# A two-layer trunk step on one core: weights loaded a stage ahead, and the second norm in the tail of the expert stage

## The reference

```python
def trunk_layer(x, mod, l, p, ctx):
    sh_a, sc_a, g_a, sh_f, sc_f, g_f = jnp.split(mod, 6, axis=-1)
    h = x * (1.0 + sc_a) + sh_a
    mix, new_ctx = token_mixer(h, l, p, ctx)        # attention, short conv, recurrent scans
    x = layer_norm(ALPHA * x + g_a * mix, ln_g[0], ln_b[0])
    h = x * (1.0 + sc_f) + sh_f
    ff = peer(h, p['peer_wq'], p['peer_keys'], p['peer_u'], p['peer_v'])
    x = layer_norm(ALPHA * x + g_f * ff, ln_g[1], ln_b[1])
    return x, new_ctx
# peer, for each token and each of 8 heads: query = h @ wq; the 16 best of 128*128 experts idx, softmax g;
#   act = gelu(h . u_tab[idx]);  y += sum over the 16 of (g * act) * v_tab[idx]
```

## Time and profile before

| | us |
|---|---|
| median of 3 runs | 7773.9 (7764.08 to 7782.03) |
| the profiled execution | 7747.34 |
| its span | 7745.5 |
| TensorE busy | 5922.2 |
| VectorE busy | 4112.1 |
| GpSimd busy | 2667.7 |
| ScalarE busy | 1916.5 |
| first layer's experts, mixer of layer 2 | from 1900.23; from 3957.68 |

### The profile page before, as it was taken

How to read it: one execution, slowest core, us unless ns; L and a number is a source line. 1 busy time by engine, 2 the same in 40 slices (tenths; PEclk the granted TensorE clock), 3 DMA queues, 4 the chain that set the end, 5 groups by cost and what they waited for, 6 DMA issues and landing times. The chain is left out here.

```text
span 7745.5 us, 97944 instructions
## 1 busy us (share of the span) xinstructions
PE 5922.2 (76%) x37744; PEld 4157.4 (54%) x37744; DVE 4112.1 (53%) x8666; ACT 1916.5 (25%) x3630; POOL 2667.7 (34%) x2848
## 2 busy tenths in 40 slices
PE   4877999786677777777658789997847777777774
PEld 4866999575333333333357679994833333333331
DVE  2358232454666666666445572425456666666664
ACT  1346211231122221222115442113212221222221
POOL 0110000100666666666501100002016666666663
PEclk8998999898899999999879899998979999899997
DMA  5011121014999999999820111110269999999996
GB/s 219 30 38 37 66 77 66 13 74 193 351 364 357 352 348 367 360 353 352 323 109 8 41 56 66 55 66 13 109 249 361 350 362 365 345 364 359 359 353 246
DMA packets 447652, 1659.85 MB, mean 214 GB/s; under 512 B 48552, under 2 KB 92264, under 8 KB 434540
## 3 DMA queue, kind: packets, MB, share of 16 engines
q0 software_dynamic: 368640, 1342.34, 45.6%
q1 hardware_dynamic: 77102, 305.91, 10.5%
q10 hardware_dynamic: 1440, 5.24, 0.2%
HBM read 1638.45 MB, written 20.10 MB: 214 GB/s over the span
## 5 line engine op out<-in xcount | busy, mean ns | idle before, releaser
L1764 PE MATMUL ex_ps_y<-early,peer_small 128*128 128x512 f32 x5120 | 2512.3, 640 | 858.3 <-DMA early<-in_peer_v,ex_index 724.1
L1764 PEld LDWEIGHTS ex_ps_y<-early,peer_small 128*128 128x128 f32 x5120 | 991.1, 203 | 2299.2 <-issue 1221.1
L1673 DVE CUSTOM_DVE_ANT_0 ring<-ring,ex_ps_h 128x1024 f32<-128x1024 f32 x1280 | 1511.1, 1218 | 744.1 <-DMA ring<-in_peer_u,ex_index 598.9
L1582 POOL DMA_INDIRECT ring<-in_peer_u,ex_index x1280 | 1219.4, 953 | 798.9 <-issue 375.3
L1582 POOL DMA_INDIRECT early<-in_peer_v,ex_index x1280 | 1219.1, 952 | 799.8 <-issue 354.5
L1724 ACT ACTIVATE peer_small<-ident,ex_w 128x128 f32<-128x128 f32 x1280 | 444.2, 393 | 1502.6 <-PE ex_ps_y L1764 668.6
L735 POOL TENSOR_TENSOR att_qs<-att_q,ring 128x512 f32<-128x512 f32 x16 | 20.2, 1264 | 1121.0 <-DMA att_lam_in<-in_lam 965.4
L911 POOL TENSOR_TENSOR room<-room,rec_bounds 128x256 f32<-128x256 f32 x80 | 69.7, 872 | 963.2 <-ACT room L905 962.9
L235 PE MATMUL conv_ps<-h_high,conv_wh 128*128 128x320 f32 x1024 | 317.6, 310 | 16.5 <-DVE conv_wl L135 16.5
L1745 PE MATMUL ex_ps_q<-h_high,ex_wh 128*128 128x256 f32 (+1 forms) x768 | 259.3, 338 | 79.8 <-DVE ex_wl L135 45.8
L235 PE MATMUL conv_ps<-h_low,conv_wh 128*128 128x320 f32 x1024 | 317.1, 310 | 0.0
(11 more groups left out here) (314 smaller groups left out, 12428.0 us busy)
## 6 DMA issues: line engine op xcount, KB each, us to landing
ring<-in_w_in SPq DMA_DIRECT2D x44, 2048.0 KB, 8.3
ring<-in_mod_w SPq DMA_DIRECT2D x16, 2048.0 KB, 15.7
ring<-in_w_branch SPq DMA_DIRECT2D x12, 2048.0 KB, 7.8
early<-in_mod_w SPq DMA_DIRECT2D x12, 2048.0 KB, 19.1
ring<-in_peer_u,ex_index POOLq DMA_INDIRECT x1280
early<-in_peer_v,ex_index POOLq DMA_INDIRECT x1280
mod_w<-in_mod_w SPq DMA_DIRECT2D x8, 2048.0 KB, 25.3
room<-in_peer_wq SPq DMA_DIRECT2D x16, 1024.0 KB
```

The source lines that it names most:

```text
L1582: nc.gpsimd.indirect_dma_start(rows[slot], None, table, bass.IndirectOffsetOnAxis(ap=index[n % 4][:, s:s + 1], axis=0)).then_inc(arrived[s ...
L1673: V.tensor_tensor_reduce(out=row, in0=row, in1=ps_h[:], scale=1.0, scalar=0.0, op0=ALU.mult, op1=ALU.add, accum_out=dot[n % 2][:, s:s + 1] ...
L1764: last = nc.tensor.matmul(ps_y[n % 2][:, c:c + 512], diag[s % DIAGS], v_row[s % V_SLOTS][:, c:c + 512], start=s == 0, stop=s == TOPK - 1)
```

## The change

1. **First weights in the stage ahead.** `projections` no longer loads its first chunk: it lies in `ring[0]` when the stage begins, and ACT's first two splits wait for nothing. Each stage ahead gets one load of 2 MB: mt ahead of `rf0` of the first layer (`w_first`, behind the x loads), the two scans (after the state's store and a wait for the 36th of 40 products on DVE), `recm` ahead of `conv` and `conv` ahead of `qkv` (argument `then`), the attention core ahead of `attm` (behind its own loads; these move from `ring[0]` to `ring[1]`), and `experts` ahead of the next layer's `rf0`. Each of these stages waits for the load before its end.
2. **The second norm in the tail of `experts`.** In the last head (units 35 to 39, `FIRST` = 35), `gather_sum` is replaced by `residual(b)`: y added into PSUM, multiplied there by the gate, ALPHA * x added, then statistics and variance of the block. `residual(0)` to `residual(3)` stand in units 36 to 39, `residual(4)` behind everything. x is loaded into the rows of h that are used up, one block per unit, the gate rows when the last query weights are split, the norm's rows after the last score.
3. **The next modulated input in the tail.** Behind the last product DVE normalises and modulates blocks 0 to 2 (`normalised`), then block 4's residual, then blocks 3 and 4; TensorE transposes, ACT copies, DVE subtracts the five blocks (`new_low_of`). The modulation rows are loaded into `ring[1]` after the last product. mt runs once, before the loop.
4. x goes straight to the outputs and is read from there; `copy_rows` is gone, and so is `residual_norm`.

The diff, cut to its core:

```diff
@@ projections
             def _(sp):
-                first = weighted[0].weights
-                for p, (k0, k1) in enumerate(pieces(0)):
-                    sp.dma_start(ring[0][:, k0:k1, 0:HALF], first[:, k0:k1, 0:HALF]).then_inc(first_loaded[p], 16)
-                sp.dma_start(ring[0][:, :, HALF:], first[:, :, HALF:]).then_inc(w_loaded[0], 16)
                 beside.load(sp)
...
                 beside.finish(sp)
+                if then is not None:
+                    sp.wait_ge(low_done, splits(2 * (len(weighted) - 2) + 1))
+                    sp.dma_start(ring[0][:], then).then_inc(next_in, 16)
+                    sp.wait_ge(next_in, 16)
@@ attention_core
-        room = ring[0][:].rearrange("p k n -> p (k n)")
+        room = ring[1][:].rearrange("p k n -> p (k n)")
...
+                sp.dma_start(ring[0][:], w_in(T, l, ZG)).then_inc(k_out, 16)
@@ scan
                 sp.wait_ge(s_done, (blocks.index(CTX_BLOCK) + 1) * HEADS)
                 sp.dma_start(T["new_state"][one, d].rearrange("a p n -> (a p) n"), state_ctx[:]).then_inc(s_out, 16)
-                sp.wait_ge(s_out, 16)
+                sp.wait_ge(x_done, UNITS - G)
+                sp.dma_start(ring[0][:], then).then_inc(s_out, 16)
+                sp.wait_ge(s_out, 32)
@@ experts, SP
+                sp.wait_ge(low_done, PH)
+                for cond in range(2):
+                    sp.dma_start(gate[:, cond, :], mod_row(T, l, cond, 5)).then_inc(gate_in, 16)
+                for b in range(NB):
+                    sp.wait_ge(rows_ready, FIRST + b + 1)
...
+                    sp.dma_start(x_tok[:, b, :], x_from(b)).then_inc(x_in, 16)
+                sp.wait_ge(scored, units)
+                for j, row in enumerate(("ln_g", "ln_b")):
+                    sp.dma_start(gb[:, j, :], ...).then_inc(gb_in, 16)
+                sp.wait_ge(u_used, TOPK * units - U_SLOTS // 2)
+                sp.dma_start(ring[0][:], w_next).then_inc(stored, 16)
+                sp.wait_ge(u_used, TOPK * units)
+                for cond in range(2):
+                    for j in range(2):
+                        sp.dma_start(vec[:, cond, j, :], mod_row(T, l + 1, cond, j)).then_inc(vec_in, 16)
+                for b in range(NB):
+                    sp.wait_ge(x_done, b + 1)
+                    sp.dma_start(x_to(b), x_tok[:, b, :]).then_inc(stored, 16)
+                sp.wait_ge(stored, 16 * (NB + 1))
@@ experts, DVE
+                def residual(b):
+                    x, ps = x_tok[:, b, :], ps_y[(FIRST + b) % 2][:]
...
+                    dve.wait_ge(v_used, TOPK * (FIRST + b + 1))
+                    tail(V.tensor_tensor(ps, ps, y_tok[:, b, :], ALU.add))
+                    tail(V.tensor_tensor(ps, ps, gate[:, b // (NB - 1), :], ALU.mult))
+                    dve.wait_ge(x_in, 16 * (b + 1))
+                    V.scalar_tensor_tensor(x, x, ALPHA, ps, ALU.mult, ALU.add).then_inc(y_out, 1)
...
-                    if n:
+                    if n > FIRST:
+                        residual(n - 1 - FIRST)
+                    elif n:
                         gather_sum(n - 1)
...
-                gather_sum(units - 1)
+                dve.wait_ge(u_used, TOPK * units)
+                dve.wait_ge(vec_in, 64)
+                tail(V.tensor_scalar(vec[:, :, 1, :], vec[:, :, 1, :], 1.0, None, ALU.add))
+                dve.wait_ge(gb_in, 32)
+                inverse(0, 0, 3)
+                for b in range(3):
+                    normalised(b)
+                residual(4)
+                new_low_of(0)
+                inverse(1, 3, 5)
+                normalised(3)
+                new_low_of(1)
+                normalised(4)
+                for b in range(2, NB):
+                    new_low_of(b)
@@ trunk
+        modulate_and_transpose(nc, 0, T, rows, h_split, ident, 0, ring)
         with nc.Fori(0, depth) as l:
-            modulate_and_transpose(nc, l, T, rows, h_split, ident, 0)
...
-                residual_norm(nc, l, T, "ln2", 1, y_tok, x_tok, rows, None, 5, rows)
-        copy_rows(nc, "end", [(T["y_sample"], T["x_rows"][0:LAT, :]), (T["y_prompt"], T["x_rows"][LAT:TOK, :])])
```

More of the change, by code:

```diff
@@ L135, in low_part, with projections @@
     return nc.vector.tensor_tensor(low, full, high.bitcast(F32), ALU.subtract)
-def projections(nc, name, jobs, ring, beside=None):
+def projections(nc, name, jobs, ring, beside=None, then=None):
     beside = beside or Beside()
@@ L949, in recurrent_out @@
         turn = Turn(o_tok, branch_split, beside.column[:, 0:1], ident)
-        projections(nc, "recm", jobs + [gates[0], turn, gates[1]] + products, ring, beside)
+        projections(nc, "recm", jobs + [gates[0], turn, gates[1]] + products, ring, beside, w_in(T, l, ZC))
 class MixerEnd(AttentionBeside):
@@ L1042, in _, with scan @@
                 last.then_inc(rows_done, 1)
-def scan(nc, l, T, d, q_t, i_tok, kk, o_tok, ring, ident):
+def scan(nc, l, T, d, q_t, i_tok, kk, o_tok, ring, ident, then):
     blocks = list(range(NB)) if d == 0 else list(range(NB - 1, -1, -1))
@@ L1509, in _, with experts @@
                 mod.add_bias(summed)
-def experts(nc, l, T, h_split, h_tok, y_tok, early, small, ident, u_in, v_in, ring):
+def experts(nc, l, T, h_split, h_tok, y_tok, early, small, ident, u_in, v_in, ring, x_from, x_to, w_next):
     units = NB * PH
@@ L1545, in experts @@
         iota, base = sb("ex_iota", [P, TOPK]), sb("ex_base", [P, DEPTH])
+        stats, mv, root = sb("ex_stats", [P, NB, 12]), sb("ex_mv", [P, NB, 2]), sb("ex_root", [P, NB])
+        x_tok = h_tok
+        gate, gb = (small[0][:, i * 2 * D:(i + 1) * 2 * D].rearrange("p (a n) -> p a n", a=2) for i in range(2))
+        vec = ring[1][:].rearrange("p k n -> p (k n)").rearrange("p (c j n) -> p c j n", c=2, j=2)
+        h_new = y_tok
+        FIRST = (PH - 1) * NB
         ps_y = [ctx.enter_context(nc.psum_tensor(f"ex_ps_y{j}", [P, D], F32)) for j in range(2)]
@@ L1730, in _ @@
                                 high(h + 2)
+                for b in range(NB):
+                    act.wait_ge(transposed, b + 1)
+                    act.activation(h_split[0][:, :, b * P:(b + 1) * P], new_psum[b % 2][:].rearrange("p (k t) -> p k t", k=KT),
+                                   ACT.Copy).then_inc(new_high, 1)
+                    if b == 0:
+                        act.wait_ge(var_done, 5)
+                        act.activation(root[:, 3:5], mv[:, 3:5, 1], ACT.Sqrt).then_inc(root_done, 1)
             @block.tensor
@@ L1781, in _ @@
                         sums(n, s)
+                for b in range(NB):
+                    pe.wait_ge(h_done, b + 1)
+                    if b == 0:
+                        pe.wait_ge(u_used, TOPK * units)
+                    elif b == 1:
+                        pe.wait_ge(y_out, units - 1)
+                    else:
+                        pe.wait_ge(new_low, b - 1)
+                    for k in range(KT):
+                        last = nc.tensor.transpose(new_psum[b % 2][:, k * P:(k + 1) * P], h_new[:, b, k * P:(k + 1) * P], ident[:])
+                    last.then_inc(transposed, 1)
 CHOICE_STEPS = 15
@@ L1789, in token_rows @@
     return lambda b: x_rows[b * P:(b + 1) * P, :]
-def copy_rows(nc, name, pairs):
-    with stage(nc, f"{name}_done") as (block, (done,)):
-        @block.sync
-        def _(sp):
-            for dst, src in pairs:
-                sp.dma_start(dst, src).then_inc(done, 16)
-            sp.wait_ge(done, 16 * len(pairs))
 def trunk(nc, T, depth=DEPTH, stop=None):
@@ L1893, in chunks @@
         return w.transpose(*range(r), r + 2, r + 1, r, r + 3)
+    w_in_chunks = chunks(a["w_in"])
     conv = np.concatenate([a["conv_w"], a["conv_b"][:, None, :]], axis=1)
```

137 lines of the change are left out of this document (55 added, 82 removed).

## The result

The changed kernel takes 7662.5 us (median of four runs, 7659.7 to 7668.8) beside 7778.0 for the kernel before on the same chip: a ratio of 0.9841, 95% interval 0.9827 to 0.9854, by the medians 115.5 us less. The forecast was 7661. The profiled execution after took 7668.84 us (span 7667.2), the slowest of its four, while the one of before (7747.34) was the fastest of its kernel; so the two traces differ by 78 us only, and a term has to be read from its stage, not from the two spans.

A forecast was written before the change was run, and what follows sets the result against it. DMA bounds the expert stage; elsewhere TensorE stands still at stage borders. Layer tail 58.1 + end 25.0 + starts 30.8 and 3.9 - scans 4.4 = 113.4 us less: 7634 profiled, 7661 median; range 7640 to 7685, with rivals 7625 to 7702.

The forecast's parts named there:

- The median: Whole run: the profiled execution lay 26.6 us below the runs' median, so 7634 becomes 7661.
- The stage starts: Projection stages: preloaded weights save 3.8 us at each of eight starts (30.8) and 3.9 at the program's first.
- The forward scan: Its load for the next stage queues behind the state's store, losing 2.2 us twice, 4.4 in all.
- (a): Expert units 36 to 38: residual work on DVE costs 11 us, moved loads 3; 14 a layer, bounds 2 and 25.
- (b): Last expert unit: next weights add 5.1 us, modulation rows 1.2, then 23.9 after TensorE; stage ends 29 later.
- The rule on the two-port operation: Expert tail: VectorE's fast +1 might block GpSimd's gather descriptors, 1.3 us a layer; sum 111 instead of 113.
- Rival C: Late expert units: moved bytes are all paid, (a) 25 a layer, modulation rows 5 later; 7692 us, chance 0.18.

The follow-up runs named there:

- scan_first: Changed kernel with the forward scan's load of the next weights issued ahead of the wait for the state and its store: 7650.1 us against 7662.5.
- own_drain: Changed kernel with one GpSimd drain added right behind its last gather, the barrier's own drain kept: 7178.7 us against 7196.3.
- after_again: The changed kernel run again with no edit, on the other chip: 7196.3 us against 7297.9 for the kernel before.
- attm_late: Changed kernel with two extra 1.95 us ScalarE copies ahead of attm's first split; that stage took 193.5 and 193.6 us, no whole time given.

## Why the prediction was right, and where only its sum was

**The median.** The step from the profiled execution's 7634 to 7661, by the 26.6 us that it lay below the median, was needed: no other run of before at this pace was as fast (all lie from 7763 to 7802), and from its trace alone the forecast would have been 28 us too low.

**The stage starts**, 8 x 3.85 = 30.8 and 3.9: the mechanism right, the size too large. The starts became 2.45 as said; the stages got shorter by 23.2 and 2.5. conv and qkv gave 4.2 and 3.6 each, recm 2.8, attm 0.9. The step that failed is that "each start earns 3.8": it took a stage's later part as unchanged and as one in which TensorE works without gaps, and in attm, which has two stalls, the matmuls ran 7.8 us longer at the lower clock. In the first start, ScalarE's table is now loaded in it (1.28 us): mt did that load inside the loop, and now it stands ahead of the loop, so the first activation in the loop's body is this start's. The start behind the loop's branch has the same:

```profile
3904.95 1.28 ACT L264 ACT_TABLE_LOAD   x1 [14.93 <-issue]
```

That is most of why it came 7.3 us behind the barrier (7.4 to 8.1 in the other traces) and not 3.9 + 2.4.

**The forward scan.** Right: +5.3 for +4.4, and scan_first shows that it is the place in SP's queue and nothing else.

**Not foreseen.** The first norm is 2.1 us longer in each layer. DMA was busy for 0.98 to 1.01 of its middle 40 us before and now; its first loads go out 0.2 us behind the barrier in both kernels, its first 2 MB load at 11.2 before and 11.6 now, and in three traces with the same code layer 0's took 84.4 to 84.6 us, nearly as before (83.8, 84.0). I have no run on it, and it stays open. Nor did the prediction see the 3.3 us of the barriers.

**(a), the late units.** 14 a layer forecast, some 13 measured on the steady chip; on the slower one units 34 to 39 take 14.2 more on average, where 19.1 was forecast with (b)'s load. But the split was wrong, and that is the step that failed here: the 4.7 MB were put at 3 and cost 8, and DVE's 13 us of residuals were put at 11 and cost less. Two of the three cost 5.3 for their 8.6 us, and moving all three gave 2.1 back. That the two errors nearly cancel is luck. I had argued that POOL's 1.60 us waits show DVE exposed and that DMA at 0.56 has room. POOL does wait 4 us longer, but not all of it reaches the next unit; that the rows in its slots absorb the rest is my reading and no run's. A stage at 0.96 over 100 us had no room that came for nothing, however low one slice of 5 us was.

**(b), the last unit.** Right nearly row by row: 2 MB cost 4.7 to 5.4 (5.1), the modulation rows 1.7 (1.2; 32.5 us from unit 39's weights to the last sum, for 30.8), 23.8 from there (23.9), the barrier 10.05 (9.8), the drain unchanged. What was taken as a fixed cost of the border, the drain, is one only where nobody does it earlier.

**The rule on the two-port operation.** The +1 over 128x2048 ran at 3849.50 for 1.23 us, and POOL's next gather at 3851.02 had waited 2.93 us, but for TensorE (the row names ex_ps_y). So no run here shows that the operation holds up a gather, nor that it doesn't; the rule's price would have changed the sum by 2.6 us.

**Small slips in the prediction's sums.** Rival C's 15.5 a layer is 16 by its own terms (25 for 14, and 5), and a row of 0.5 MB each 1.73 us is 303 GB/s, not 305; neither moves the forecast.

**Left open.** The terms read from stages give 98.9 us, close to the 101.7 measured on the steady chip (90 to 112 by its ratio) and below the slower one's 115.5 (114 to 135). There the expert stages of one and the same kernel differ by 17 us from one execution to the next (2064.1 and 2081.5 in layer 0), and no trace shows which part of the rest is the change's. The prediction hit 7661 within 2 us; its terms were off by 14.5 in sum, and that the slower chip gave back as much is luck.

## What to carry to other kernels

A load that is hidden at one place costs its bytes at another: in a stage at 0.96 DMA the 4.7 MB cost 8 us a layer and the 2 MB some 5, and the 2 MB became nearly free only behind the last rows of both streams. Read a stage's end, not only its start: a start about 4 us earlier shortened its stage by anything from 0.9 to 4.2 us. And where a barrier waits for an engine's drain, let that engine drain itself at its own last instruction, while the others still work.

## What the runs showed of the hardware

- GpSimd's drain behind 1280 indirect DMAs a layer takes 8.545 to 8.547 us even when it begins 34.7 us after the last gather's end (3856.9 to 3891.6). So it isn't waiting for the gathers' transfers, whose last rows TensorE had summed by 3867.5; it is work that waits to be done, once (own_drain). What work, no run shows. The next drain takes 34 ns.
- Two chips run the same program 6.6% apart (7297.9 and 7778 us), nearly all of it in the expert stage: 41.8 us and some 48 a unit of 16.8 MB, 401 and 350 GB/s. The faster repeats nearly every unit within 1 us (2.4 at most), the slower scatters by 20 over 34 units in one kernel. What sets them apart no run shows.
- A 2 MB load takes 8.0 us from issue to landing as the median of 54, 10.4 in the expert stage beside the row gathers, and 15.3 in the stage ahead of the loop, issued right behind nine loads of 0.5 MB (after_again: the whole run, 3575 to 3600 us, 100 to 125 us):

```profile
ring<-in_w_in SPq DMA_DIRECT2D x54, 2048.0 KB, 8.0
...
ring<-in_w_first SPq DMA_DIRECT2D x1, 2048.0 KB, 10.4
...
ring<-in_w_first SPq DMA_DIRECT2D x1, 2048.0 KB, 15.3
```

- Behind one and the same stall of 3.21 us TensorE's granted clock stayed at 1.00 in both traces of before and fell to half in every other, in attm_late with the stall at the same place in the stage. It also fell behind a stall of 2.69 us (0.82 over 8 us).
- A branch back to the head of the loop held TensorE's queue for 3.8 us (after, 3901.60 to 3905.36).
